# Loading, squaring and normalising the latent tokens ahead of the context tokens in the first phase of a two-block kernel

## The reference, cut to what matters

```python
D_MODEL = 1024; SEQ = 256; CTX_LEN = 256; EPS = 1e-6
# first block, layer 0
sc_lat, sc_ctx = silu(c), silu(c_ctx)
m_l = sc_lat @ w_ada + b_ada          # 6 * 1024 columns, shift and scale first
m_c = sc_ctx @ w_ada + b_ada
hl = rmsnorm(x, g) * (1 + scale_l) + shift_l      # latent tokens
hc = rmsnorm(ctx, g) * (1 + scale_c) + shift_c    # context tokens
v = [hc; hl] @ w_in[:, values]        # the first product of the kernel
# second block
h = rmsnorm_2(x, pre_mix_norm); proj = h @ w_in_2       # its value columns are computed first
```

## Time and profile before

| what | value |
|---|---|
| median of 3 runs | 875.49 us (875.2 to 875.95) |
| the profiled execution: its own time | 874.96 us |
| the profiled execution: span from first to last instruction | 873.1 us |
| mean granted TensorE clock | 0.998 |
| TensorE matmul busy | 863.6 us (99%) |
| VectorE busy | 641.5 us (73%) |
| ScalarE busy | 488.5 us (56%) |
| first value matmul starts | 19.92 us |

### The profile page before, as it was taken

One profiled execution on the slowest core, in us unless ns is written; L12 is line 12 of the kernel. 1 busy time (PEld: TensorE's weight loads), 2 busy tenths in 40 slices (PEclk: granted clock), 3 DMA queues, 4 the chain that ended last, 5 costly groups with the idle time before them and its releaser, 6 DMA issues.

```text
span 873.1 us, 16932 instructions
## 1 busy us (share of the span) xinstructions
PE 863.6 (99%) x6308; PEld 783.7 (90%) x6308; DVE 641.5 (73%) x1080; ACT 488.5 (56%) x769; POOL 0.2 (0%) x4
## 2 busy tenths in 40 slices
PE   8999999999999999999999999999999999999997
PEld 3688888888899999999998899999998899999996
DVE  3793899999997787877677897766577765555555
ACT  5433677777766664655557545555544664444443
POOL 0000000000000000000000000000000000000000
PEclk9999999999999999999999999999999999999999
DMA  9974444444447556565564654444465465555551
GB/s 343 408 285 158 145 146 146 143 144 144 160 143 252 185 202 242 170 216 186 175 191 143 196 193 146 150 165 146 145 218 171 140 200 195 185 192 185 180 188 48
DMA packets 45585, 160.90 MB, mean 184 GB/s; under 512 B 5216, under 2 KB 6624, under 8 KB 45408
## 3 DMA queue, kind: packets, MB, share of 16 engines
q1 hardware_dynamic: 43632, 156.43, 52.7%
q10 hardware_dynamic: 1904, 3.81, 1.3%
HBM read 159.16 MB, written 1.05 MB: 183 GB/s over the span
## 4 chain that ended last, share of the span: by engine, by line
PE 94%; DVE 2%; ACT 1%; DMA 1%; SPq 0%; issue 0%; DVEq 0%; ACTq 0%
PE bank L420 22%; PE bank L422 21%; PE bank L421 21%; PE bank L474 5%; PE bank L476 5%; PE bank L475 5%; PE bank L1224 2%; PE bank L1227 2%; PE bank L1225 2%; DMA tok<-in_tok 1%; PE bank L442 1%; PE bank L1315 1%; PE bank L1333 1%; PE bank L1195 1%; PE bank L1296 0%; DVE arena L657 0%
## 5 line engine op out<-in xcount | busy, mean ns | idle before, releaser
L414 DVE TENSOR_TENSOR w_lo<-raw,w_hi 128x1024 fp32r<-128x1024 f32 x244 | 295.2, 1223 | 118.0 <-ACT w_hi L407 117.9
L420 PE MATMUL bank<-h_hi,w_hi 128*128 128x256 f32 (+1 forms) x1168 | 350.1, 300 | 0.0
L422 PE MATMUL bank<-h_hi,w_lo 128*128 128x256 f32 (+1 forms) x1168 | 343.5, 294 | 0.0
L421 PE MATMUL bank<-h_lo,w_hi 128*128 128x256 f32 (+1 forms) x1168 | 343.4, 294 | 0.0
L407 ACT ACTIVATE w_hi<-raw 128x1024 fp32r<-128x1024 f32 x244 | 252.7, 1051 | 111.3 <-PE bank L422 82.9
L420 PEld LDWEIGHTS bank<-h_hi,w_hi 128*128 128x128 f32 x1168 | 219.5, 188 | 9.5 <-issue 0.8
L421 PEld LDWEIGHTS bank<-h_lo,w_hi 128*128 128x128 f32 x1168 | 220.3, 189 | 6.5
L422 PEld LDWEIGHTS bank<-h_hi,w_lo 128*128 128x128 f32 x1168 | 220.0, 188 | 5.8
L420 PE MATMUL bank<-y_hi,w_hi 128*128 128x256 f32 x304 | 87.0, 286 | 0.1
L421 PE MATMUL bank<-y_lo,w_hi 128*128 128x256 f32 x304 | 85.6, 282 | 0.0
L422 PE MATMUL bank<-y_hi,w_lo 128*128 128x256 f32 x304 | 85.5, 281 | 0.0
(11 more groups left out here) (272 smaller groups left out, 1100.5 us busy)
## 6 DMA issues: line engine op xcount, KB each, us to landing
raw<-in_stream SPq DMA_DIRECT2D x244, 512.0 KB, 3.4
arena<-in_ada SPq DMA_DIRECT2D x40, 512.0 KB, 7.2
xres<-in_ada SPq DMA_DIRECT2D x8, 512.0 KB, 3.3
tok<-in_tok SPq DMA_DIRECT2D x3, 512.0 KB, 7.7
con<-in_con ACTq DMA_DIRECT2D x1, 1472.0 KB, 7.1
xres<-in_tok ACTq DMA_DIRECT2D x1, 1024.0 KB, 10.1
out<-arena SPq DMA_DIRECT2D x4, 256.0 KB, 2.0
tok<-in_tok SPq DMA_DIRECT2D x2, 256.0 KB, 9.5
```

Source lines behind the costliest of these rows:

```text
L414: dve.tensor_tensor(w_lo[c.slot][:, :], raw[c.slot][:, :], w_hi[c.slot][:, :].bitcast(F32), ALU.subtract).then_inc(S("split_lo"), 1)
L420: pe.matmul(dst, hi_w, a_hi, start=start, stop=False, skip_group_check=True)
L421: pe.matmul(dst, hi_w, a_lo, start=False, stop=False, skip_group_check=True)
L422: return pe.matmul(dst, lo_w, a_hi, start=False, stop=stop, skip_group_check=True)
```

## The change

The tokens are laid out anew: `tok` (and the array in memory that it is loaded from) now holds all eight column tiles of the latent tokens and then all eight of the context tokens. The pieces become latent tiles 0 to 3, latent 4 to 7, context 0 to 3, context 4 and 5, context 6 and 7. The norm is computed for latent tokens first and for context tokens later, into two PSUM banks (1 and 2). TensorE's value matmuls are cut into single tiles with waits of their own, and their order in the first chunk is new. In the second block three weight splits stand at earlier places.

The core of the diff:

```diff
-PIECES = (0, 2, 4, 6, 7, 8)
+PIECES = (0, 4 * T, 8 * T, 12 * T, 14 * T, 16 * T)
...
+def made_at(k, half):
+    return 2 * half + k + 1 if k < 2 else 2 * k + half + 1
...
+            load_tokens(0)
             load_ada(0)
+            load_tokens(1)
             load_ada(1)
-            load_tokens(0)
             load_ada(2)
-            load_tokens(1)
+            load_ada(3)
+            sp.dma_start(par[:, :], par_in).then_inc(S("par_in"), 16)
+            load_one(0)
             load_tokens(2)
-            load_ada(3)
             load_tokens(3)
             load_tokens(4)
-            load_one(0)
-            sp.dma_start(par[:, :], par_in).then_inc(S("par_in"), 16)
...
-            for n in range(5):
-                square_piece(n)
-            copy_rows(0)
-            hi(act, Chunk(0))
-            act.wait_ge(S("tok_summed"), 4)
+            square_piece(0)
+            square_piece(1)
             act.wait_ge(S("eps"), 1)
             log_sum(0)
             root(0)
+            copy_rows(0)
+            hi(act, Chunk(0))
+            modulate_half(0, 0)
+            square_piece(2)
+            modulate_half(1, 0)
+            square_piece(3)
+            square_piece(4)
             log_sum(1)
-            modulate_half(0, 0)
             root(1)
             modulate_half(0, 1)
-            modulate(1)
             copy_rows(1)
+            modulate_half(1, 1)
             hi(act, Chunk(1))
...
-            act.dma_start(by_tile(xres[:, :]), by_tile(tok_in)[:, :, 0:T]).then_inc(S("xres_in"), 16)
+            act.dma_start(xres[:, :], tok_in[:, 0:KT * T]).then_inc(S("xres_in"), 16)
...
-            square_residual(act, 1)
-            for k in range(2, 6):
+            square_residual(act, 1, 0, KT // 2)
+            hi(act, Chunk(N_IN2, 2 + AHEAD))
+            square_residual(act, 1, KT // 2)
+            for k in range(3, 6):
                 hi(act, Chunk(N_IN2, k + AHEAD))
...
+            def add_tokens(bank, first, start, stop):
+                for m in range(2):
+                    last = pe.matmul(psum[bank][:, 0:T], ones, wide[:, first + m * T:first + (m + 1) * T],
+                                     start=start and m == 0, stop=stop and m == 1, skip_group_check=True)
+                return last
+            def context_sum():
+                pe.wait_ge(S("tok_added"), 4)
+                add_tokens(2, PIECES[2], True, False)
+                pe.wait_ge(S("tok_squares"), 5)
+                add_tokens(2, PIECES[4], False, True).then_inc(S("tok_summed"), 1)
...
-            ada(0, 2)
             warm(FILL[0])
-            ada(2, 3)
-            token_sum(0)
+            pe.wait_ge(S("tok_added"), 1)
+            add_tokens(1, PIECES[0], True, False)
+            ada(0, 1)
+            pe.wait_ge(S("tok_added"), 2)
+            add_tokens(1, PIECES[1], False, True).then_inc(S("tok_summed"), 1)
+            ada(1, 4)
             warm(FILL[1])
-            token_sum(1)
-            ada(3, 4)
-            token_sum(2)
             pe.wait_ge(S("con_in"), 16)
             turn_rows(0)
-            token_sum(3)
-            ada(4, 5)
             warm(FILL[2])
-            values(0, {(0, 1): lambda: ada(5, 8), (0, 3): lambda: turn_rows(1)})
+            value_tile(0, 0, 0)
+            value_tile(0, 0, 1)
+            value_tile(0, 1, 0)
+            context_sum()
+            value_tile(0, 1, 1)
+            ada(4, 7)
+            value_tile(0, 0, 2)
+            ada(7, 8)
+            value_tile(0, 0, 3)
+            value_tile(0, 1, 2)
+            turn_rows(1)
+            value_tile(0, 1, 3).then_inc(S("multiplied"), 1)
...
+            add_squares(1, PIECES[0], PIECES[0] + 2 * T)
+            add_squares(2, PIECES[1], PIECES[1] + 2 * T)
+            for k in range(0, KT, 2):
+                norm_tokens(k, 0)
             dve.wait_ge(S("par_in"), 16)
             quarter(0)
+            shift_half(0, 0)
             lo(dve, Chunk(0))
-            norm_half(0, 0)
-            norm_half(1, 0)
-            shift_half(0, 0)
             low_half(0, 0)
-            norm_half(0, 1)
+            add_squares(3, PIECES[2], PIECES[2] + 2 * T)
+            shift_half(1, 0)
+            dve.wait_ge(S("tok_added"), 3)
+            add_squares(4, PIECES[2], PIECES[3])
+            low_half(1, 0)
+            norm_tokens(0, 1, 1)
             shift_half(0, 1)
-            norm_half(1, 1)
+            norm_tokens(1, 1, 1)
             low_half(0, 1)
-            shift_tokens(1)
-            low_tokens(1)
-            norm_tokens(2)
-            norm_tokens(3)
+            shift_half(1, 1)
+            low_half(1, 1)
             quarter(1)
...
             for m in range(KT):
-                if m in (2, 5):
+                if m in (2, 4, 6):
                     lo(dve, Chunk(N_IN2, m // 2 + 1 + AHEAD))
                 add_weighted_squares(dve, m)
-            lo(dve, Chunk(N_IN2, 4 + AHEAD))
             for m in range(1, KT):
-                if m == 4:
+                if m == 3:
                     lo(dve, Chunk(N_IN2, 5 + AHEAD))
```

More of the change, by code:

```diff
@@ L531, in wait_residual, with square_residual @@
             engine.wait_ge(S("residual"), update * KT + m + 1)
-        def square_residual(act, update):
-            for m in range(KT):
+        def square_residual(act, update, first=0, end=KT):
+            for m in range(first, end):
                 wait_residual(act, update, m)
@@ L1211, in turn_rows, with value_tile @@
                 last.then_inc(S("mod_turned"), 1)
+            def value_tile(j, b, tile):
+                c, half = Chunk(j), j // 4
+                k = 2 * (j % 4) + b
+                x = slice(k * TC + tile * P, k * TC + (tile + 1) * P)
+                dst = psum[4 * half + tile][:, :]
+                hi_w, lo_w = (w[c.slot][:, b * 512:b * 512 + 512] for w in (w_hi, w_lo))
+                pe.wait_ge(S("split_hi"), c.n + 1)
+                pe.wait_ge(S("h_hi"), made_at(k, tile // 2))
+                pe.matmul(dst, h_hi[:, x], hi_w, start=k == 0, stop=False, skip_group_check=True)
+                pe.wait_ge(S("split_lo"), c.n + 1)
+                pe.matmul(dst, h_hi[:, x], lo_w, start=False, stop=False, skip_group_check=True)
+                pe.wait_ge(S("h_lo"), made_at(k, tile // 2))
+                last = pe.matmul(dst, h_lo[:, x], hi_w, start=False, stop=k == KT - 1, skip_group_check=True)
+                if k == KT - 1 and tile < 3:
+                    last.then_inc(S("v_bank"), 1)
+                return last
             def values(j, between={}):
-                c, half = Chunk(j), j // 4
-                pe.wait_ge(S("split_lo"), c.n + 1)
                 for b in range(2):
-                    k = 2 * (j % 4) + b
                     for tile in range(4):
-                        x = slice(k * TC + tile * P, k * TC + (tile + 1) * P)
-                        dst = psum[4 * half + tile][:, :]
-                        hi_w, lo_w = (w[c.slot][:, b * 512:b * 512 + 512] for w in (w_hi, w_lo))
-                        pe.wait_ge(S("h_hi"), 2 * k + 1 + tile // 2)
-                        pe.matmul(dst, h_hi[:, x], hi_w, start=k == 0, stop=False, skip_group_check=True)
-                        pe.matmul(dst, h_hi[:, x], lo_w, start=False, stop=False, skip_group_check=True)
-                        pe.wait_ge(S("h_lo"), 2 * k + 1 + tile // 2)
-                        last = pe.matmul(dst, h_lo[:, x], hi_w, start=False, stop=k == KT - 1, skip_group_check=True)
-                        if k == KT - 1 and tile < 3:
-                            last.then_inc(S("v_bank"), 1)
+                        last = value_tile(j, b, tile)
                         if (b, tile) in between:
@@ L1740, in low_half @@
                 x = slice(k * TC + half * T, k * TC + (half + 1) * T)
[L1741 to L1743 removed]
+                dve.wait_ge(S("tok_shifted"), made_at(k, half))
+                dve.wait_ge(S("h_hi"), made_at(k, half))
+                dve.tensor_tensor(h_lo[:, x], wide[:, token_cols(k, half)], h_hi[:, x].bitcast(F32), ALU.subtract).then_inc(S("h_lo"), 1)
             def low_tokens(k):
@@ L1778, in _ @@
             low_half(2, 0)
+            norm_tokens(2, 1)
             shift_half(2, 1)
```

52 lines of the change are left out of this document (26 added, 26 removed).

## The result

| kernel | median us | lowest to highest (executions) | ratio to before, 95% interval |
|---|---|---|---|
| before | 875.49 | 875.2 to 876.36 (6) | |
| changed | 878.69 | 878.03 to 880.05 (6) | 1.0035 [1.0023, 1.0047] |

The account below looks back on a forecast made before the run. TensorE, 99% busy, was taken as the bound, so the head's shift moves the end: -2.9 lead, +2.95 moved work, +3.55 waits, taken as +3.5, less 0.06, on 875.49 gives 878.9 us; range 877.0 to 880.2.

Parts of the forecast that it names:

- The new start: Head of the kernel: first value matmul at 17.0 us instead of 19.92, 2.9 us earlier.
- The context sum: TensorE, now behind the first value matmul: four fp32 matmuls of 256 columns add 1.9 us.
- The lone chunk: TensorE, behind the new start: adaLN chunk 7 alone, with a change of matmul kind, adds 1.05 us.
- Wait 1: First value tile: second and third matmuls wait for `w_lo` and `h_lo`, 0.85 us together.
- Wait 2: Third matmul of latent tile 1, third tile in order: waits 0.5 us for `h_lo` from VectorE.
- Wait 3: Context root and its `h_hi`: ready at 24.5 us, TensorE busy to 25.0; no wait, 0.5 in hand.
- Wait 4: Third context tile in order: its `h_hi` stands behind quarter 1's row copy on ScalarE, 0.5 us.
- Wait 5: Head of value chunk 1: only one tile follows quarter 1's transposition, so three matmuls wait, 1.7 us.
- The clock falls: Rival: less matmul work in 16 to 20 us drops the clock to half, adding 3 to 4 us, 882; chance 4%.
- No new waits: Rival: latent tiles run freely and chunk 1 finds its inputs, only -2.9 + 2.95 remains, 875.5 us; chance 7%.
- the lead is kept: Rival: quarter 0's reduction starts at 12.8 us, chunk 7 and context sum fill the waits, 872.7 us; chance 3%.
- Splits and residual DMA: Second block: earlier weight splits save 0.06 us; the residual's DMA, now reading whole rows, changes nothing.

Follow-up runs that it names:

- chunk 7 joined: Changed kernel with adaLN chunk 7 in one group with chunks 4 to 6: median 876.84 us, ratio 1.0019 to the kernel before.
- sums behind: Changed kernel, chunk 7 grouped, quarter 1's transposition early, context sums after latent tiles: 875.59 us with its fills, 875.61 with six and six, 874.55 and 874.79 without early fills.
- changed again: The changed kernel run once more, unaltered, for the spread of its times: 878.05 to 879.84 us, ratio 1.0032 to the kernel before.
- no fills: Changed kernel without the six fill matmuls ahead of the latent sum: 878.64 us, ratio 1.0030 to the kernel before.
- transposition earlier: Changed kernel with chunk 7 joined and the transposition of quarter 1 moved behind the first context tile: 876.45 us, ratio 1.0006 to the kernel before.
- half of the sum: Changed kernel with two of the context sum's four matmuls left out: 878.77 us, ratio 1.0029 to the kernel before.
- set 2: Runs on one chip, from the repeated changed kernel to six fills in the wait and the first kernel with sums behind; kernel before there 875.80 us.
- set 3: Runs on another chip: the other kernels with sums behind, and one with context squares added on VectorE; kernel before there 875.30 us.
- splits-alone run: Kernel before with only the second block's weight splits moved: 875.58 us against 875.68, ratio 0.9998.

## Why the prediction was right, step by step

- **What bounds the kernel**: right. After the four-chunk group the two traces run side by side to 0.1 us as far as the second block; moving the head moved the end.
- **The new start** (17.0, a lead of 2.9): 16.33 in one execution, 17.02 in another. That no transfer holds it was right. The prediction had two chains meet at 15.6, the transposition and the normalisations; the normalisations come last, by 0.2. What I took as fixed, 7.68 for TensorE to be free and 1.53 for six fills, both from one trace, varies: the twelve zero matmuls took 2.94, 2.98, 3.13, 3.46, 3.60 and up to 4.05 us. Where they are quick the start was forecast 0.7 too late.
- **The context sum** (1.9): 1.54. I charged a step of 0.98 for two matmuls of 256 columns; four in a chain take 0.39 each. Mis-sized by 0.35.
- **The lone chunk** (1.05): 25.95 - 24.96 = 0.99 and 0.1 for the changes. Shown by its removal, with wait 4: together 1.8 us in the trace and 1.7 between the shortest times.
- **Wait 1** (0.85): 0.83. **Wait 2** (0.5): 0.46. **Wait 3** (none, 0.5 in hand): none. **Wait 4** (0.5): 0.54. **Wait 5** (1.7): 0.94 and 0.83, 1.77. Of these, 5 was taken away by itself, all but 0.55 of it, on top of the kernel with chunk 7 joined; 2 is gone only in the kernels with sums behind, with other edits; 1 was never undone and is read from the trace alone. The steps between tiles and other matmuls, 0.4 us, stood in no term of the sum but for 0.1.
- **The sum** (+3.5 at the group): +2.92 in the profiled execution of 878.2, and 33.74 - 29.55 = +4.19 in the one of 879.48. The forecast of 878.9 is close to the median of 878.69 partly by luck: a start forecast too late and a context sum forecast too long worked against a clock forecast too steady and steps left out.
- **The clock falls** (4%, 3 to 4 us): this was under-weighed and over-priced. Of seven profiles of kernels with two fills in the wait, the changed kernel and its variants, five show the fall (changed again, no fills, chunk 7 joined, transposition earlier, half of the sum) and two do not (the changed kernel's first, sums behind). None of the five with six fills in the wait shows it. Four of those five have the sums behind too, an order in which the one profile with two fills shows no fall either, so the profiles alone leave a rival. The mean granted clock of every execution settles more: it is 0.997 or less in 16 of 57 executions with two fills in the wait and in none of 50 with six; the kernel before has one in 79. In set 2 that is 4 of 12 against 0 of 17, in set 3, with the sums behind in all, 2 of 11 against 0 of 33. (0.998 does not tell: a fall behind the last matmul gives it too.) Its price is 0.6 us in the execution of 879.48 and up to 1.0 in the others, since the tiles stretch into waits that are there anyway. My argument gave 2.7 us of matmuls to the stretch from 16 to 20 us, and that was near (3.08 in the profiled execution); but the sparse stretch is the one from 14 to 18, with 1.06 and 1.28 of 4 us.
- "The trace before shows no such drop" holds only for its head. At its end the clock falls to 0.50 from about 870.3 us on, behind the last matmul, which ends at 867.8; there it costs nothing. That fall is what makes its mean 0.998.
- **No new waits** and **the lead is kept**: both out. Taking waits 2 and 4, most of 5 and the lone chunk away gives 875.6 with the fills of the changed kernel, level with the kernel before, and 874.3 to 874.8 with the early fills gone and six in the wait, 0.5 to 1.3 under the kernel before of the same set (in one of the three runs the 95% interval of the ratio includes 1). But no run made quarter 0 start near the 12.8 us that the second rival needed: in the best of them its reduction is at 14.6.
- **Splits and residual DMA** (-0.06 and nothing): right. The DMA now lands 5.2 us after its issue instead of 10.1, and nobody waited for either.

Why the clock fell in some executions and not in others of one kernel stays open, and so does why the zero matmuls are slow in some. Among the profiles with early fills and two fills in the wait the two go together (a fall with 3.46 to 4.05 us for the twelve, none with 2.94 and 3.13), so part of the distance between short and long executions, 2.0 us between the middles of the two groups with chunk 7 joined, is late fills and not the fall. More matmuls ahead of the wait take the fall away but not the median: it is equal with and without them (878.61 and 878.73; 875.59 and 875.61).

## What to carry to other kernels

An earlier start of the bounding engine is worth only what remains after the work carried across the start and after the waits that the shorter covers create: here 3.6 us of lead paid for 2.5 us of moved work and 3.6 us of waits. Measure each producer's chain from the event that starts it to the instruction that needs it, and count how many microseconds of other matmuls stand between them in the new order. And matmuls of zeros that keep the engine busy are harmless only as long as something else is slower. Put on the path, they hand on whatever they vary by: here 2.94 to 4.05 us for the same twelve, with the first value matmul 8.04 to 8.05 us behind the sum that follows them each time.

## What the runs showed of the hardware

- The granted clock fell to 0.50 although TensorE was never idle for longer than about 1.3 us just before: in the execution of 879.48 the last fills end at 15.75, the next matmul is at 17.02, and it runs at the lower level. A mean clock of 0.998 hides this; the kernel before has the same mean from a fall behind its last matmul.
- Matmuls at the start ran slowly in a stretch for which the rows give a granted clock of 1.00: twelve zero matmuls of the same shapes took from 2.94 to 4.05 us. In the slowest profile (chunk 7 joined) those from 5.7 to 6.9 us have weight loads of 333 ns in the middle and matmuls of 421 ns, where the changed kernel has 192 and 276. That is what a lower clock would do, but no row shows one there; it is my reading.
- A load of 1 MB in whole rows landed in 5.1 to 6.5 us in twelve profiles, where the one in pieces of 256 columns took 10.1 and, in the splits-alone run, 9.0. Other loads ran beside them.
